# Sixteen cache copies issued from ScalarE's queue instead of SyncE's, and one weight block moved to a buffer of its own

## The reference, cut to what matters

```python
h = rmsnorm(x);  qa,ka,va,qb,kb,vb,qc,gate_logits = split(h @ w_in)     # w_in 1024 x 5376
mk, mv = split(rmsnorm(mem) @ w_mem_kv)                                 # for the prompt
oa = window_attention(qa, ka, va, sink)                                 # 8 heads, window 128
ob = dilated_attention(qb, kb, vb)                                      # 12 heads, 3 dilations
oc = memory_attention(qc, mk, mv)                                       # 4 heads, 256 memory tokens
x  = x + (sig(g0)*(oa @ w_br_a) + sig(g1)*(ob @ w_br_b) + sig(g2)*(oc @ w_br_c)) @ w_out
x  = x + moe(rmsnorm(x))            # 32 experts, top 4, w_gate_up 1024 x 2048, w_down 1024 x 1024 each
# for the samples the caches are also returned, moved by the 4 new rows:
dil_k_s = concat(cache_dil_k, kb)[:, -2048:]      # (8, 2048, 4, 64); dil_v_s and swa_k_s, swa_v_s alike
```

## Time and profile before

| | us |
|---|---|
| median of 3 runs | 1280.77 |
| the profiled execution | 1281.79 |
| its span | 1280.0 |
| PE busy in the span | 1212.1 (95%) |
| DVE / ACT / POOL busy | 417.3 / 233.8 / 74.4 |
| moved by DMA | 502.37 MB, mean 392 GB/s |

### The profile page before, as it was taken

One profiled execution on the slowest core, in us unless ns is written; L12 is line 12 of the kernel. 1 busy time (PEld: TensorE's weight loads), 2 busy tenths in 40 slices (PEclk: granted clock), 3 DMA queues, 4 the chain that ended last, 5 costly groups with the idle time before them and its releaser, 6 DMA issues.

```text
span 1280.0 us, 14766 instructions
## 1 busy us (share of the span) xinstructions
PE 1212.1 (95%) x6122; PEld 512.7 (40%) x6122; DVE 417.3 (33%) x919; ACT 233.8 (18%) x459; POOL 74.4 (6%) x79
## 2 busy tenths in 40 slices
PE   9979999999999999999999999999999989899996
PEld 4446667666533333333333333333333333233332
DVE  3274653325442313223142322213131422222233
ACT  2211534230210111201112110111111110101012
POOL 0570002400200000000000000000000000000000
PEclk9989999999999999999999999999999999999998
DMA  9989899799799999999999999999999999999994
GB/s 340 383 272 362 306 357 359 240 300 421 281 387 389 429 428 427 428 428 428 429 428 427 429 428 427 427 429 428 428 429 429 427 428 427 429 428 429 429 426 178
DMA packets 74792, 502.37 MB, mean 392 GB/s; under 512 B 6992, under 2 KB 31184, under 8 KB 49104
## 3 DMA queue, kind: packets, MB, share of 16 engines
q1 hardware_dynamic: 72864, 497.10, 95.9%
q0 software_dynamic: 848, 2.36, 0.5%
q10 hardware_dynamic: 1008, 1.90, 0.4%
HBM read 498.42 MB, written 37.03 MB: 418 GB/s over the span
## 4 chain that ended last, share of the span: by engine, by line
PE 62%; DMA 31%; DVE 4%; SPq 1%; issue 1%; ACT 1%; DVEq 0%; ACTq 0%
PE ps L1801 20%; DMA ring<-in_w_gate_up 17%; PE ps L1840 10%; DMA tail<-in_w_gate_up 7%; DMA late<-in_w_gate_up 7%; PE ps L1274 6%; PE ps L1190 4%; PE ps L1757 4%; PE ps L1701 3%; PE ps L1551 2%; PE ps L1564 2%; PE ps L1818 1%; PE ps L1252 1%; PE ps L1720 1%; DMA ring<-in_w_mem_kv 1%
## 5 line engine op out<-in xcount | busy, mean ns | idle before, releaser
L1801 PE MATMUL ps<-ring,cq 128*64 128x512 f32 x1232 | 280.1, 596 | 20.5 <-DMA ring<-in_w_gate_up 20.5
L1801 PEld LDWEIGHTS ps<-ring,cq 128*64 128x64 f32 x1232 | 83.9, 136 | 191.3 <-issue 144.9
L1840 PE MATMUL ps<-ring,cq 128*64 128x512 f32 x592 | 134.3, 595 | 0.7 <-issue 0.7
L1274 PE MATMUL ps<-arena,ring 128*128 128x288 f32 x384 | 102.3, 412 | 2.0 <-ACT ring L933 2.0
L1074 ACT ACTIVATE cq<-ps 128x512 f32<-128x512 f32 x32 | 19.1, 597 | 451.0 <-PE ps L1818 451.0
L2336 DVE TENSOR_REDUCE tail<-ps 128x1 f32<-128x288 f32 x15 | 6.9, 457 | 286.2 <-PE ps L1733 286.2
L1274 PEld LDWEIGHTS ps<-arena,ring 128*128 128x128 f32 x384 | 69.6, 189 | 25.6 <-issue 4.9
L1190 PE MATMUL ps<-ring,arena 128*128 128x512 f32 (+3 forms) x240 | 72.3, 555 | 0.3 <-DMA ring<-in_w_in 0.3
L1840 PEld LDWEIGHTS ps<-ring,cq 128*64 128x64 f32 x592 | 41.0, 136 | 73.3 <-issue 69.8
L2364 DVE TENSOR_TENSOR x_tok<-x_tok,ps 64x512 f32<-64x512 f32 (+2 forms) x51 | 43.8, 860 | 70.2 <-PE ps L1757 64.7
L1088 ACT ACTIVATE cq<-ps 64x512 f32<-64x512 f32 x32 | 18.8, 589 | 230.3 <-PE ps L1840 230.3
(11 more groups left out here) (388 smaller groups left out, 1326.3 us busy)
## 6 DMA issues: line engine op xcount, KB each, us to landing
ring<-in_w_gate_up SPq DMA_DIRECT2D x77, 2048.0 KB, 42.2
ring<-in_w_down SPq DMA_DIRECT2D x37, 2048.0 KB, 43.7
tail<-in_w_gate_up SPq DMA_DIRECT2D x13, 2048.0 KB, 41.0
late<-in_w_gate_up SPq DMA_DIRECT2D x12, 2048.0 KB, 41.8
cq<-in_w_gate_up SPq DMA_DIRECT2D x12, 2048.0 KB, 42.3
arena<-in_w_gate_up SPq DMA_DIRECT2D x12, 2048.0 KB, 42.7
ring<-in_w_in SPq DMA_DIRECT2D x9, 2048.0 KB, 11.0
out_dil_k_s<-in_cache_dil_k SPq DMA_DIRECT2D x8, 2044.0 KB
```

Source lines behind the costliest of these rows:

```text
L1274: ins = pe.matmul(bank(gate_bank(m))[:, 0:TT], wblk[(6 + m // 4) % 2][:, k, (m % 4) * P:(m % 4 + 1) * P], hT_v[:, k, :], start=(k == 0), s ...
L1801: ins = pe.matmul(bank(gu0 + u)[64 * h:64 * h + 64, :], xTe[:, k % 4, (k // 4) * 64:(k // 4) * 64 + 64], pair_buf[slot][:, a:a + 512], sta ...
L1840: ins = pe.matmul(bank(7 if last else 5)[64 * h:64 * h + 64, :], aT[:, kk % 4, (kk // 4) * 64:(kk // 4) * 64 + 64], pair_buf[slot][:, a:a ...
```

## The change

Three things change together. First, block 4 has an area of its own, 2048 columns of the tile `late` that later hold the prompt's probabilities; the blocks after it swap areas (block 5 now follows block 2 in area 0, block 6 follows block 3 in area 1, and from there the two alternate). The rotary embedding's scratch moves from there to `pT`, and two expert buffers swap places in `pair_buf`. Second, the sixteen copies are issued by ACT. Third, PE's waits before the sample scores are split: `k_transposes(0)` starts when the last transposed probabilities are evicted, the second group waits for `o_evicted`.

```diff
+        wblk.append(probs.rearrange("p (k n) -> p k n", n=256))
...
         W_QKV, W_MEM, W_GATE, W_BR = range(5), 5, range(6, 12), (12, 13)
+        AREA = [0, 1, 0, 1, 2] + [1 - i % 2 for i in range(5, 14)]
...
             def load_wblk(i):
-                dst, s = wblk[i % 2], S[f"wblk{i % 2}_in"]
-                if i >= 2:
-                    wait_wblk_used(sp, i - 2)
+                dst, s = wblk[AREA[i]], S[f"wblk{AREA[i]}_in"]
+                if AREA[i] in AREA[0:i]:
+                    wait_wblk_used(sp, max(j for j in range(i) if AREA[j] == AREA[i]))
...
             load_wblk(3)
-            copy_cache()
-            copy_cache()
             load_wblk(4)
...
+            def copy_caches(count):
+
+                for _ in range(count):
+                    x, b = copies.pop(0)
...
+                    act_e.dma_start(dst.rearrange("(a n) -> a n", a=64), src.rearrange("(a n) -> a n", a=64)) \
+                        .then_inc(S["copy_dma"], 16)
...
+                copy_caches((0, 2, 0, 1, 2)[n])
                 if n == 1:
                     act_e.wait_ge(S["rstd"], 2)
...
+            copy_caches(1)
...
             for u in range(0, NU, 2):
                 final = u + 2 == NU
+                copy_caches({0: 2, 4: 3, 8: 3}.get(u, 0))
                 evict_gate()
...
                 evict_kt(act_e, b, 1, lambda o, i: act_e.activation(o, i, ACT.Copy), "kta_evicted")
+            copy_caches(2)
...
-            pe.wait_ge(S["o_evicted"], NU)
-            pe.wait_ge(S["exp_done"], NU)
+            pe.wait_ge(S["pt_evicted"], NU)
             def k_transposes(b):
...
+                    if g == 2:
+                        pe.wait_ge(S["o_evicted"], NU)
...
             k_transposes(0)
+            pe.wait_ge(S["exp_done"], NU)
...
-            tmp = probs
+            tmp = pT[:, 384:1024]
```

More of the change, by code:

```diff
@@ L268, in build @@
         W_QKV, W_MEM, W_GATE, W_BR = range(5), 5, range(6, 12), (12, 13)
+        AREA = [0, 1, 0, 1, 2] + [1 - i % 2 for i in range(5, 14)]
         wblk_dmas = [4 if i in W_BR else 1 for i in range(14)]
         def wblk_ready(eng, i):
-            eng.wait_ge(S[f"wblk{i % 2}_in"], 16 * sum(wblk_dmas[i % 2:i + 1:2]))
+            eng.wait_ge(S[f"wblk{AREA[i]}_in"], 16 * sum(wblk_dmas[j] for j in range(i + 1) if AREA[j] == AREA[i]))
         def wait_wblk_used(eng, i):
@@ L441, in build @@
         r_cmp = area(early, 0, NOV, NE)
-        pair_buf = [late[:, 0:2 * SLOT], cq[:, NINTH:NINTH + 2 * SLOT], tail[:, 0:2 * SLOT]] + [ring[:, 2 * SLOT * i:2 * SLOT * (i + 1)] for i in (0, 1, 4, 5, 2, 3)] + \
+        pair_buf = [late[:, 0:2 * SLOT], cq[:, NINTH:NINTH + 2 * SLOT], tail[:, 0:2 * SLOT]] + [ring[:, 2 * SLOT * i:2 * SLOT * (i + 1)] for i in (1, 0, 4, 5, 2, 3)] + \
             [arena[:, MASKS:MASKS + 2 * SLOT]]
@@ L512, in load_wblk @@
                     sp.dma_start(dst[:, 6:8, :], d["w_br_c"][0].rearrange("(m p) n -> p m n", p=P)[:, :, n]).then_inc(s, 16)
[L514 to L524, removed]
             def recent_rows(src):
@@ L713, in _ @@
             load_pair(2)
-            while copies:
-                copy_cache()
             for i in W_BR:
@@ L861, in roots @@
                 act_e.activation(norm_st[:, 8 + a:8 + b], norm_st[:, a:b], ACT.Sqrt, bias=norm_st[:, 6:7]).then_inc(S["root"], 1)
+            copies = [(x, b) for x in ("k", "v") for b in range(NB_S)]
+            def copy_caches(count):
+                for _ in range(count):
+                    x, b = copies.pop(0)
+                    n = (LB - NQ_S) * 256
+                    src = d[f"cache_dil_{x}"][0, b].rearrange("r h n -> (r h n)")[NQ_S * 256:]
+                    dst = d[f"dil_{x}_s"][0, b].rearrange("r h n -> (r h n)")[0:n]
+                    act_e.dma_start(dst.rearrange("(a n) -> a n", a=64), src.rearrange("(a n) -> a n", a=64)) \
+                        .then_inc(S["copy_dma"], 16)
             act_e.wait_ge(S["v_self"], 2)
@@ L1018, in _ @@
             act_e.activation(PR_C, SC_C, ACT.Exp, bias=s_st[:, 1:2], accum_out=s_st[:, 5:6]).then_inc(S["s_exp"], 1)
+            assert not copies
             evict_gate()
@@ L1190, in proj_products @@
                     ins = pe.matmul(bank((n % 2) * 3 + t)[k_rows(t, k), 0:b - a],
-                                    hT_v[:, k, TOK0[t]:TOK0[t] + NTOK[t]], wblk[n % 2][:, k, 0:b - a],
+                                    hT_v[:, k, TOK0[t]:TOK0[t] + NTOK[t]], wblk[AREA[n]][:, k, 0:b - a],
                                     **k_group(t, k))
@@ L1251, in _ @@
                 for k in range(KC):
-                    ins = pe.matmul(bank(3 + t), memT[:, k, t * P:(t + 1) * P], wblk[1][:, k, :],
+                    ins = pe.matmul(bank(3 + t), memT[:, k, t * P:(t + 1) * P], wblk[AREA[W_MEM]][:, k, :],
                                     start=(k == 0), stop=(k == KC - 1))
@@ L1273, in gate_products @@
                 for k in ks:
-                    ins = pe.matmul(bank(gate_bank(m))[:, 0:TT], wblk[(6 + m // 4) % 2][:, k, (m % 4) * P:(m % 4 + 1) * P],
+                    ins = pe.matmul(bank(gate_bank(m))[:, 0:TT], wblk[AREA[6 + m // 4]][:, k, (m % 4) * P:(m % 4 + 1) * P],
                                     hT_v[:, k, :], start=(k == 0), stop=(k == KC - 1))
@@ L1551, in _ @@
                         ins = pe.matmul(bank(3 * (dt % 2) + br)[:, 0:TT],
-                                        wblk[blk % 2][:, k, (dt % 4) * P:(dt % 4 + 1) * P], oT[:, k, :],
+                                        wblk[AREA[blk]][:, k, (dt % 4) * P:(dt % 4 + 1) * P], oT[:, k, :],
                                         start=(k == ks[0]), stop=(k == ks[-1]))
```

14 lines of the change are left out of this document (1 added, 13 removed).

## The result

The changed kernel takes 1320.21 us (median of 4 runs, 1314.02 to 1321.32), the kernel before 1281.42 us beside it: ratio 1.0282, 95% interval 1.0264 to 1.0300. It is slower, as forecast, but by 38.8 us and not by 9; 1320 lies outside the range of 1279 to 1308. The profiled span is 1318.2 us against 1280.0.

What follows compares the result with a forecast made beforehand. PE was taken to bound the front, DMA the expert stage. Terms: 0 (block 3) + 2 (memory block) + 8 (blocks 9 and 10) + 0.3 (ACT's time) - 0.9 (split wait) = +9.4 us, forecast 1290 us, range 1279 to 1308.

Steps and rivals of the forecast that it cites:

- What bounds it: Whole kernel: PE paces the front, DMA the expert weights; a shift of PE in front moves the end by the same.
- Block 4 in its own area: Block 4's load: no longer waits for block 2, but PE never waited for block 4; 0 us.
- How two queues share: DMA engines: one packet for one packet, so each 65 KB copy packet lets one 2 KB packet of SP's queue through.
- Place 1: Block 3: two copies overtake it, PE stands 6.8 us, taken from the memory block's 7.1 us wait; cost 0.
- Place 2: Memory block: one copy meets part of its packets; 2 us, from 0 to 5.7, or 12 if two more copies pass.
- Place 3: Blocks 9 and 10: sets of three copies make them 4.8 and 8.1 us late, not added; 8 us, bounds 0 and 11.8.
- The clock: PE after stalls: a few matmuls at the lower clock, said to be in the rounding.
- The split wait: Before the sample scores: 7 of 14 transposes run in the idle time before them; -0.9 us, said as -1.
- No harm: Rival: queues share by bytes or by runs, blocks land in time, only -0.9 to +1.5 us stays; 1280 us, chance 0.20.
- Faster: Rival: memory block lands 3.9 us sooner without a copy behind it, -5 us in all; 1276 us, chance 0.10.
- Overtaken twice: Rival: copies 11 to 13 also pass block 9, about 20 us late, +22 or +32; 1303 to 1313 us, chance 0.15.

Runs made afterwards that it cites:

- the first experiment: The changed kernel with the sixteen copies back in SyncE's list at their old places; 1284.48 us, ratio 1.0009 against the kernel before.

## Why the prediction was right in sign and wrong in size

- **What bounds it, and that the front shifts the end one for one: right.** 38.1 us in the front, 38.2 in the span.
- **Block 4 in its own area: 0, right**, by the first experiment (1.0009). The prediction did not see that the same exchange makes an earlier memory block possible.
- **How two queues share: right.** 51 to 54, 112 to 112. The Trainium skill (DMA: Bandwidth & Descriptors, "Queues, rings and completion order") has typically 9 to 17 descriptors in a turn; that is not what these rows show.
- **Place 1, block 3: right.** 6.8 us were predicted, 7.4 measured, and taken from the memory block's wait; leaving copies 1 and 2 out gained nothing. But the stall also kept copies 3 to 5 behind the memory block. Without it that block is waited for 23.2 us, 16 more than before, and block 6 no longer. The 12 us that the prediction allowed for this case were too few.
- **Place 2, the memory block, + 2: the step that failed first.** The memory block was not late at all (issued at 83.12, landed 9.9 us later, nothing waited). The next load in SP's queue was. I looked at the block a copy stood beside and not at block 6, issued 2.5 us later, which three copies and then a fourth overtook: 12.8 us, confirmed by leaving copies 3 to 5 out. Block 6 was counted nowhere, though the trace of the kernel before shows how close it was: there it landed at 103.0 us and was wanted at 108.9, a slack of 5.9 us, and three copies hold the engines for 17.
- **Place 3, blocks 9 and 10, + 8: mis-sized, 21.9.** The steps were worked out for one overtaking. The second set, 17 us more, stood in a rival with 0.15, as a matter of 2 us. It was less close than that: of the first set, issued from 171.60, no packet moved before 174.3 and its last ended at 194.3, 22.7 us and not 17.0 after the issue, while the next set came 21.2 us after it. Block 9, issued 3 us behind the first set, could not be done by then: its first packet moved at 192.05, behind dot keys of its own queue that had crept along with the copies. 18 of the 21.9 us go when the second set goes. The stall at block 6 has no part in it, for without that stall the wait is 22.8 us. Block 10, to which the prediction had given its 8 us, was not waited for.
- **The clock: put at nothing, 5.0 us.** "In the rounding" was wrong for three stalls. From 219.4 to 232 us, behind the longest, the granted clock is 0.78 in the mean, part of that stretch at the lower of its two levels, and the front's matmuls take 5.0 us more.
- **The split wait, - 0.9: measured 0.8 at its place.** With the copies in SP's queue it gave 0 in the time, since DVE was next; in the changed kernel that wait for DVE is gone too.
- **The rivals.** No harm is excluded. Faster is excluded, although its idea, that an earlier landing of the memory block is worth some us, holds (6.8 us) once the block itself is moved. Overtaken twice is what happened, at two places: it gave 1303 to 1313, the chip 1320. Its second place was not its own: it had 12 us at the memory block, and the chip 12.8 at block 6.

The sum with the measured terms is 0.3 (block 3 less the memory block) + 12.8 + 21.9 - 0.8 + 5.0, 39.2 us, against 38.1.

## What to carry to other kernels

Two queues share by packets, so a transfer of large packets in a second queue all but stops the small ones of the first until it is done: go through every load in the first queue from the copy's issue to its end, not only the one beside it, and through the issues behind them, since a late block is overtaken by the next set too. A transfer that nobody reads belongs behind the urgent one in the same queue; of the eight kernels here that issued all sixteen from another queue, in pieces of 65 KB, none came nearer to the kernel before than 1.2%. When a wait is taken away, look which engine is next.

## What the runs showed of the hardware that was not expected

- Copies from DRAM to DRAM in pieces of 2044 bytes move 145 GB/s, in aligned pieces of 2048 bytes 344, in pieces of 65 KB 369. The Trainium skill (DMA: Bandwidth & Descriptors, "Specifications") gives 512 bytes as the least for full rate; all pieces here are above that, and those of 2044 bytes moved at less than half the rate of the others.
- A queue that is nearly stopped holds its issuing engine: SP needed 16.31, 18.43 and 18.49 us for one or two small DMAs.
- A newcomer in the second queue starts a little later beside a backlog in the first: the first packet of the copies issued at 45.39 and 171.60 us moved 4.4 and 2.7 us later, that of the copies issued at 146.65 and 265.42 us 1.4 and 1.3. The set of 171.60, put at 17 us of work, ran 19.9 us from its first packet and so ended 22.7 us after its issue.
